# Moving the embedding projection of a one-core transformer-layer kernel from its last stage into its routing stage

## What is computed

```python
def channel_and_ple(x, p, g_ffn, w_rg, b_rg, w_re, b_re, w_gate, w_up, w_down, g_ple, w_ple_gate, w_ple_proj):
    h = rmsnorm(x, g_ffn).reshape(B * S, D)
    x = x + hier_moe(h, w_rg, b_rg, w_re, b_re, w_gate, w_up, w_down).reshape(B, S, D)
    e = (p.astype(x.dtype) @ w_ple_proj) * jax.nn.sigmoid(rmsnorm(x, g_ple) @ w_ple_gate)
    return x + e
...
y_prompt = rmsnorm(xp, final_norm_g)
```

## Time and profile before

| quantity | value |
|---|---|
| profiled execution | 2257.42 us, span 2255.6 us |
| median of the three runs | 2261.59 us |
| PE busy | 1997.7 us (89% of the span) |
| DVE, ACT, POOL busy | 1129.8, 867.4, 238.2 us |
| routing stage (e) | 1401.8 to 1431.5 us of the span |
| last stage (h) | 2064.6 to 2255.6 us of the span |

### The profile page before, as it was taken

How to read it: one execution, slowest core, us unless ns; L and a number is a source line. 1 busy time by engine, 2 the same in 40 slices (tenths; PEclk the granted TensorE clock), 3 DMA queues, 4 the chain that set the end, 5 groups by cost and what they waited for, 6 DMA issues and landing times. The chain is left out here.

```text
span 2255.6 us, 26518 instructions
## 1 busy us (share of the span) xinstructions
PE 1997.7 (89%) x9556; PEld 1633.7 (72%) x9556; DVE 1129.8 (50%) x1339; ACT 867.4 (38%) x1014; POOL 238.2 (11%) x232
## 2 busy tenths in 40 slices
PE   7889999965999999997999895499999999993887
PEld 5767888854777777786788684377777777773676
DVE  4224333324232233211643432789999999994443
ACT  4222000011332333322421211477777777773443
POOL 0000111122000000000222000100000000002232
PEclk9999999987999999987999897699999999996999
DMA  8426111197777545465333336399999999985231
GB/s 286 154 103 233 52 61 60 40 322 255 259 260 265 205 156 187 151 216 199 150 126 110 118 112 253 138 339 397 390 394 396 392 395 391 397 308 208 99 119 68
DMA packets 190913, 494.02 MB, mean 219 GB/s; under 512 B 16512, under 2 KB 32384, under 8 KB 180352
## 3 DMA queue, kind: packets, MB, share of 16 engines
q1 hardware_dynamic: 180128, 457.69, 55.4%
q0 software_dynamic: 7200, 26.22, 3.2%
q10 hardware_dynamic: 3520, 9.25, 1.1%
HBM read 402.94 MB, written 90.18 MB: 219 GB/s over the span
## 5 line engine op out<-in xcount | busy, mean ns | idle before, releaser
L2223 DVE TENSOR_TENSOR expert_w_rounded<-arena,expert_w_rounded 128x2048 fp32r<-128x2048 f32 x192 | 431.7, 2288 | 47.8 <-ACT expert_w_rounded L2180 47.8
L2180 ACT ACTIVATE expert_w_rounded<-arena 128x2048 fp32r<-128x2048 f32 x192 | 360.1, 1912 | 60.6 <-PE psum L162 39.1
L160 PE MATMUL psum<-expert_w_rounded,expert_x_rounded 128*128 128x512 f32 x768 | 312.1, 406 | 34.2 <-DVE expert_x_rounded L2236 27.1
L162 PE MATMUL psum<-expert_w_rounded,expert_x_rounded 128*128 128x512 f32 x768 | 303.1, 395 | 0.0
L161 PE MATMUL psum<-expert_w_rounded,expert_x_rounded 128*128 128x512 f32 x768 | 302.1, 393 | 0.0
L160 PE MATMUL psum<-host_w_rounded,host_x_rounded 128*128 128x512 f32 x432 | 195.1, 452 | 15.1 <-ACT arena L888 8.2
L160 PEld LDWEIGHTS psum<-expert_w_rounded,expert_x_rounded 128*128 128x128 f32 x768 | 146.2, 190 | 75.3 <-issue 36.8
L162 PE MATMUL psum<-host_w_rounded,host_x_rounded 128*128 128x512 f32 x432 | 175.3, 406 | 0.0
L161 PE MATMUL psum<-host_w_rounded,host_x_rounded 128*128 128x512 f32 x432 | 174.8, 405 | 0.0
L162 PEld LDWEIGHTS psum<-expert_w_rounded,expert_x_rounded 128*128 128x128 f32 x768 | 145.8, 190 | 32.4
L161 PEld LDWEIGHTS psum<-expert_w_rounded,expert_x_rounded 128*128 128x128 f32 x768 | 146.4, 191 | 28.3
(11 more groups left out here) (288 smaller groups left out, 3654.8 us busy)
## 6 DMA issues: line engine op xcount, KB each, us to landing
arena<-w_gate_e SPq DMA_DIRECT2D x32, 2048.0 KB, 9.6
arena<-w_up_e SPq DMA_DIRECT2D x32, 2048.0 KB, 10.6
arena<-w_down_e SPq DMA_DIRECT2D x32, 2048.0 KB, 9.4
host_x_rounded<-hx_scratch SPq DMA_DIRECT2D x54, 1024.0 KB, 5.4
y_scratch<-arena SPq DMA_DIRECT2D x49, 512.0 KB, 9.7
arena<-w_in SPq DMA_DIRECT2D x10, 2048.0 KB, 10.3
z_scratch<-arena SPq DMA_DIRECT2D x54, 256.0 KB, 2.1
arena<-x_all SPq DMA_DIRECT2D x18, 512.0 KB, 4.7
```

What stands on the lines that cost most here:

```text
L160: nc.tensor.matmul(out, x_hi, w_hi, start=first, stop=False)
L162: return nc.tensor.matmul(out, x_lo, w_hi, start=False, stop=last)
L2180: nc.scalar.activation(c.exact(his[n][:, half, :]), halves[b][n][:, half, :], ACT.Copy).then_inc(*w_hi_ready[n].inc)
L2223: nc.vector.tensor_tensor(c.exact(raw), raw, c.high(his[n][:, half, :]), ALU.subtract).then_inc(*w_lo_ready[n].inc)
```

## The change

1. The projection `p @ w_ple_proj` is done in stage e, for all nine tiles: PE transposes and multiplies, ACT rounds and evicts, POOL subtracts, and ACT's own DMA queue stores the result in a new scratch tensor `emb`. Its weight and all of `p` are loaded and the weight is split in stage d. PE puts tiles 0 to 2 ahead of the count matmuls, 3 to 6 between them and the selection, 7 and 8 behind it.
2. Stage d issues its last two stores first and then only two of the six expert loads. The other four are issued at the start of stage e.
3. Stage h loads `emb` (512 KB for each tile) in place of `p` (128 KB). Its loops are written out. `combined` runs one tile further ahead (in iteration t for tile t+1), with three buffers for `x2`; the norm of t+1 is made in iteration t too. `x` keeps two buffers, and SP's order stays load(t+2), `f_ready(t)`, store(t).

```diff
             sp.wait_ge(*wo_done(NT - 1))
-            for n, (dst, src, sem) in enumerate(first):
-                if n == 1:
-                    turn(NT, 1, False, True)
+            turn(NT, 1, False, True)
+            for dst, src, sem in c.first_experts[0:2]:
                 sp.dma_start(dst, src.rearrange("(k p) n -> p k n", p=P)).then_inc(sem, 16)
...
         @block.sync
         def _(sp):
             s.credit(sp)
+            for dst, src, sem in c.first_experts[2:]:
+                sp.dma_start(dst, src.rearrange("(k p) n -> p k n", p=P)).then_inc(sem, 16)
...
+            p_high(0)
             act.wait_ge(*exp_in(0))
             nc.scalar.activation(gexp, g4, ACT.Exp).then_inc(*gap_exp.inc)
-            act.wait_ge(*gap_ready(0))
-            nc.scalar.activation(gap, gap, ACT.Exp).then_inc(*gap_exp.inc)
+            for t in range(NT):
+                if t + 1 < NT:
+                    p_high(t + 1)
+                if t == 2:
+                    act.wait_ge(*gap_ready(0))
+                    nc.scalar.activation(gap, gap, ACT.Exp).then_inc(*gap_exp.inc)
+                evict(t)
+            act.wait_ge(*emb_stored(NT - 1, 0))
+            act.wait_ge(*emb_stored(NT - 2, 1))
...
+                nc.gpsimd.tensor_tensor(c.exact(pT[:, b]), pT[:, b], c.high(pT_hi[:, b]), ALU.subtract).then_inc(*p_lo_ready.inc)
...
+            def embedded(t):
+                b = t % 2
+                if t + 1 < NT:
+                    rows_transposed(t + 1)
+                pe.wait_ge(*p_lo_ready(t))
+                pe.wait_ge(*emb_out(t - 2))
+                for h in range(2):
+                    cols = slice(h * BANK, (h + 1) * BANK)
+                    for k in range(KP):
+                        last = split_product(nc, ps[:, 4 + 2 * b + h, :], c.exact(pT_hi[:, b, k, :]), c.exact(pT[:, b, k, :]),
+                                             c.w_pp_hi_x[:, k, cols], c.w_pp_x[:, k, cols], k == 0, k == KP - 1)
+                last.then_inc(*emb_done.inc)
...
+            for t in range(NT):
+                if t + 2 < NT:
+                    load(t + 2)
                 sp.wait_ge(*f_ready(t))
-                sp.dma_start(row(c.o["y_all"], t), out[:, b]).then_inc(*out_stored.inc(b))
-            in_pairs(sp, NT, tile, peel=3)
+                sp.dma_start(row(c.o["y_all"], t), out[:, t % 2]).then_inc(*out_stored.inc(t % 2))
...
+                dve.wait_ge(*emb_in(t, t % 2))
+                dve.wait_ge(*gate_out(t, h + 1))
+                nc.vector.tensor_tensor(e[:, cols], g[:, cols], emb[:, t % 2, cols], ALU.mult).then_inc(*e_ready.inc)
+                dve.wait_ge(*e_ready(t, h + 1))
+                dve.wait_ge(*f_ready(t - 1))
+                nc.vector.tensor_tensor(x3[:, cols], e[:, cols], x2[:, t % 3, cols], ALU.add).then_inc(*x3_ready.inc)
...
+            for t in range(NT + 1):
+                if t:
+                    embedded(t - 1, 0)
+                if t + 1 < NT:
+                    combined(t + 1)
+                if t < NT:
+                    transposed(t)
+                if t + 1 < NT:
+                    mean_square(t + 1)
+                if t:
+                    embedded(t - 1, 1)
...
+            for t in range(NT + 1):
+                if t:
+                    gated(t - 1, 0)
+                if t < NT:
+                    high(t)
+                if t + 1 < NT:
+                    square(t + 1)
+                    normalized(t + 1)
+                if t:
+                    gated(t - 1, 1)
```

More of the change, by code:

```diff
@@ L1998, in _ @@
             nc.tensor.matmul(ps[:, 1, 0:NT * NE], T["ones"], rows, start=True, stop=True).then_inc(*counted.inc)
+            for t in range(3, 7):
+                embedded(t)
             for n in range(TOP * NT):
@@ L2003, in _ @@
             last.then_inc(*ids_done.inc)
+            for t in range(7, NT):
+                embedded(t)
         @block.vector
@@ L2553, in turn @@
-            def turn(t, b, new, old):
-                if new:
-                    combined(t, b)
-                if not old:
-                    w_lo(range(3, len(pieces)))
-                if old:
-                    embedded(t - 1, 1 - b, 0)
-                if new:
-                    dve.wait_ge(*gate_done(t - 2))
-                    dve.wait_ge(*emb_done(t - 2))
-                    transposed(t, b)
-                if old:
-                    embedded(t - 1, 1 - b, 1)
+                dve.wait_ge(*emb_in(t, t % 2))
```

268 lines of the change are left out of this document (139 added, 129 removed).

## The result

| | median, us | lowest to highest | profiled execution | its span |
|---|---|---|---|---|
| before | 2258.11 (20 runs) | 2255.41 to 2264.47 | 2257.42 | 2255.6 |
| changed | 2262.44 (20 runs) | 2259.39 to 2270.9 | 2264.53 | 2262.7 |

The ratio is 1.0019, with an interval of 1.0011 to 1.0027: 0.2% slower, inside the 0.3% that the prediction called no change. The prediction was 2277 us, 2263 to 2292, with a chance of 0.81 for slower. The direction was right, but by the prediction's own bound of 0.3% this is its third rival, "the same", to which it gave 0.07, and not the slower kernel to which it gave 0.81. The waits and their order came as described; the size did not: on the profiled executions the change costs 7.1 us and not 15.6. The median of before was also 3.5 us lower over 20 runs than over the 3 to which the prediction added its sum.

A forecast was written before the change was run, and what follows sets the result against it. The prediction held that no engine is full and a ring of waits bounds stage h's turn. Routing 1.2 us later plus stage h 14.4 longer made 15.6, added to the median of 2261.59: 2277 us, range 2263 to 2292.

The forecast's parts named there:

- third rival: Whole kernel: landing at 3.4 us (7 less) and routing 6 less leave 2.6 us, 2264, within the bound; chance 0.07.
- barrier before routing: End of stage d: with fewer loads issued before the barrier, routing starts at 1387.0, a gain of 14.8 us.
- stage e: Routing stage: with the projection in it, it takes 45.7 us with its barrier, where it took 29.7.
- six turns: Stage h, iterations 2 to 7: each waits for its load of x, 6 x 21.3 = 127.8 us.
- The ring: Stage h: chain of waits per turn, with the load of x behind the store that waits for POOL's gain; 21.0 us.
- PE's path: Stage h: PE starts a gate half slow after nearly 7 us idle, half 7.9 us; with handover a turn takes 21.3.
- sign for the ring: Stage h: DVE would idle some 5 to 6 us before `combined`, with the load of `x_scratch` as releaser.
- The low end: Stage h: a landing of x at the shortest, 3.4 us, gives 7 us less.
- the uncovered case: Stage d: the weight split before DVE's first residual, costed at nothing, would be 2 us if uncovered.
- POOL's subtracts: Routing stage: they slow DVE's chain by 0.5 us for each of four, 2 us, between 0 and 4.
- the page's rule alone: Routing stage: by the skill's exclusion rule, nine subtracts could each hold DVE for their full length, some 7 us.
- second rival: Routing stage: PE stays at half clock, tiles cost 5.5 us in place of 3.2, 18 us more, 2295; chance 0.08.

The follow-up runs named there:

- experiment 1: Changed kernel with SP's load of x(t+3) issued ahead of its wait for the gain in the last stage; 2239.08 us, ratio 0.9925.
- experiment 4: Changed kernel with expert 1's three loads issued only after tile 6 of the projection; 2266.83 us, ratio 1.0037.
- experiment 8: Changed kernel with all six expert loads issued in stage d, as in the kernel before; 2281.91 us, ratio 1.0094.
- experiment 5: The kernel of experiment 1 with two buffers for x3; 2239.98 us, ratio 0.9914.
- experiment 6: The kernel of experiment 5 with the next tile's first sigmoid ahead of the scaling n3 on ACT; 2240.85 us, ratio 0.9918.
- experiment 9: Kernel before with late expert loads, early tile and early x load, and the projection in PE's idle time in the last stage; 2223.33 us, ratio 0.9846.
- experiment 2: Kernel before with only the late issue of expert loads (stores first, four loads moved to stage e); 2241.52 us, ratio 0.9925.
- experiment 3: Changed kernel with the last stage's order of before, combined(t) in iteration t, still loading emb; 2247.72 us, ratio 0.9961.

## Why the prediction was wrong

Every term of the sum, on the profiled executions:

| term | predicted, us | measured, us |
|---|---|---|
| stage d, the weight's load and split | 0 | +1.7 |
| barrier before routing | -14.8 | -15.2 |
| stage e | +16.0 | +15.1 |
| stages f and g | 0 | +0.1 |
| first sigmoid of stage h, beyond that | +2.0 | +1.8 |
| iteration 1, sigmoid to sigmoid | 15.1 long | 14.7 long |
| six turns | 127.8 long | 119.6 long |
| from there to the last gain | 23.3 long | 23.1 long |
| whole execution | +15.6 | +7.1 |

**The step that failed is the size of the turn**, "With the handover I take 21.3 for a turn". It measured 19.9. Two things are in this. The ring, which the prediction had at 21.0, measured 19.8; and the prediction then took PE's path, 21.3, as the bound, where PE was on no chain that set the turn. The waits, their order and their places were as described, and experiment 1, which takes that one wait away, gives 21 us back. From the gain at 2134.93 to the next at 2154.69, with a for the sigmoid at 2135.01:

- From the gain's start to `combined` it is 6.96 us, not 7.6. SP issues the load 0.40 us after the gain's end, not 0.78, and it lands in 4.14 us, not 4.5. The 0.78 holds 0.26 us between SP's two issues in the old loop and a load of `p` that the new one doesn't have. Why the landing was shorter no run shows; the medians are 4.3 us (3.8 to 5.6) here and 4.5 (3.4 to 5.1) before. Over the six turns this part is 6.9 to 7.5 us.
- From `combined` to ACT's high parts it is 4.47 us, not 4.67; the norm to the second half's sigmoid 2.97, not 3.15; from there to `x3` 2.14, where 2.1 was foretold; the final norm and POOL's start 3.22, not 3.45. The sum is 19.8 in place of 21.0.
- PE starts the half at 2147.20, 1.1 us ahead of the prediction, and needs 7.9 us from there with its handover, where 8.0 was foretold, the first ten matmuls at the slow pace. ACT's sigmoid of that half is at 2155.11, 0.49 us late for PE, but POOL's gain at 2154.69 did not wait for it. In four turns this sigmoid waited 0.16, 0.49, 0.84 and 1.11 us for PE, and the gains behind them still came 19.7 to 19.9 us apart.

That makes 1.4 us in the mean of six turns, 8.2 us of the 8.5 by which the sum was off. An error in a turn counts six times: issue and landing, less the 0.06 that the gain took longer, are 0.7 us in a turn and 4 us in the whole, a quarter of the forecast of 15.6.

Two of the prediction's own readings were loose, too. Its sign for the ring was DVE idle for "some 5 to 6 us" before `combined`; it was 3.3 to 3.8 us. Its own numbers give 3.9 (`x3` done at a + 4.0, `combined` at a + 7.9), and part of that time the product fills, which is held by the gain. And the gain of 3.15 us is 0.81 over 2.34; 0.88 is what line 2521 had left.

**The low end was there and got too little weight.** The prediction gave "a landing at the shortest here, 3.4" as 7 us less, which is a turn of 20.2. The measured turn lies past that end, but by several small parts: the landings were 4.1 to 4.6 us in the six turns, and none was as short as 3.4. The base, a median of three runs, was 3.5 us too high as well. On the base of 20 runs the same sum would have given 2274 and a range from about 2260, in which 2262 lies. The rest is the spread between executions: the profiled one of the kernel before lies 0.7 us below its median and that of the changed kernel 2.1 above, so that the medians are 4.3 us apart and the profiled executions 7.1.

**Stage d was not free.** DVE, "before DVE's first residual, where PE has a tile's matmuls to do", waits 4.20 us for ACT's half of the split and then takes 2.29:

```profile
1261.62 2.29 DVE L1906 TENSOR_TENSOR embed_w_rounded<-arena,embed_w_rounded 128x2048 fp32r<-128x2048 f32 x1 [4.20 <-ACT embed_w_rounded L1852]
...
1265.70 0.68 DVE L1879 TENSOR_TENSOR arena<-psum,arena 128x512 f32<-128x512 f32 x1
```

The residual that started at 1262.61 before starts at 1265.70. DVE was early there by less than the split takes, and I had not looked at how much. The stage ends 1.7 us later, about the 2 that the text named for the uncovered case. That this split is the whole of the 1.7 was not tried by itself, and the size varies: from the split of `out_w` to routing's first instruction it is 137.0 to 137.8 us in the four traces without the new split, 137.8 to 137.9 in three with it and 139.3 to 139.7 in five with it. So it costs from almost nothing to some 2 us.

**Routing was right in its sum, not in all its parts.** With three tiles ahead of it the count came 14.7 us into the stage, against 15.4. But PE was not the whole reason. DVE, on its way to the count, waits 3.93 us for ACT, which does its second exponential (line 2034) only behind the evictions of the first two tiles, and then only 0.50 us for PE:

```profile
1401.06 0.70 DVE L2118 TENSOR_SCALAR arena<-arena 128x9 f32<-128x9 f32 x1 [3.93 <-ACT arena L2034]
```

The prediction had no term for this order on ACT, and no run changed it. From the count to the end of the selection's inputs it took 16.8 us, not 15.2: the chain was slowed by 1.6 us, where the prediction took 2 for POOL's subtracts, and the 7 that it worked out by the page's rule alone did not come. PE left the slow clock after six matmuls and not after twelve, so the second rival was far off. The stores landed in 6.6 us (median) and not 2.9, with the expert loads in the queues beside them; ACT waited for them three times, 2.81, 3.46 and 3.84 us. But experiments 4 and 8 show that these waits cost nothing: the selection and what comes behind it bound the stage. This error lay on a way that didn't matter. The store's 2.9 at the stage's end was a little short too; 3.63 us pass there.

The Trainium skill, DMA: Bandwidth & Descriptors, "Queues, rings and completion order", says that each DMA engine takes turns between the queue rows it has work for, a packet at a time. The traces agree as far as the sharing goes: with all four expert loads in the queues the stores took 6.6 us (median), in experiment 4, where three came late, 4.6, and in experiment 8, with none, 2.6. That it goes by packets no run here shows.

**The port.** In the table of the turn the product of line 2613 takes 2.16 us beside the gain. The prediction had the gain held by DVE (up to 5 us more) and not DVE by the gain. In the changed kernel that hold costs nothing, for DVE then waits on `x` anyway; in experiment 1 the product is recorded 1.65 us longer, and experiments 5 and 6 show that neither a buffer nor a new order removes the hold. Not all of it is lost: `x3` waits for the gain anyway, so that the turn is 0.5 us shorter without it (experiment 9). The Trainium skill, SBUF — State Buffer, "Who interferes with whom", says that this exclusion needs two SBUF inputs on VectorE, and that an instruction with at most one, outside the 2-port performance modes, does not contend. By that rule, the traces agree: with both inputs in SBUF the product takes 1.20 to 2.44 us in the changed kernel and always ends 0.53 to 0.55 us after the gain does; with one in PSUM it takes 0.69 us beside a gain of the same length (experiment 9). So staging the projection in memory had a price that no term named: it turned a free product into a held one.

**Where the gain of a large change went.** The late issue brings 15 to 17 us (experiments 2 and 8). The projection's move costs 15.1 us in routing and up to 2 in stage d, while some 7 come back in the last stage, most of them with the table loads (from SP's first load there to the last gain it is 185.6 us before and 178.5 in experiment 3). The early tile, in the order as written, costs 13 and would give 8 with one load moved up. Together that is 4 to 8 us slower; the profiled executions say 7.1 and the medians 4.3.

## What to carry over

When an operation is moved a turn earlier, look first at which queue entry now has to come a turn earlier too: here one load behind a store on SP made a gain of 8 us a loss of 13. A large change that measures as no change is worth taking apart, since a part of 15 to 17 us was in it, hidden by two that cost. Work for an engine that idles inside its loop can be free: with twelve matmuls in the gap the turn was 15.9 us, without them 16.4, while the nine tiles' projection cost 15 us as work of its own in the routing stage. And a busy share or a mean clock that moves says nothing yet about the turn: PE went to 79 of 82 us at the full clock, and what made the turn shorter was a product that no longer stood behind POOL's gain. The chain that ended last shows which of the two it is.

## What the runs showed of the hardware

- PE's clock can fall after the work has begun. In experiment 6, behind 3.22 us of idle time, the first matmuls from 2134.59 on are 0.23 us apart (2.4 GHz), those from 2136.47 to 2139.03 0.43 apart (1.2 GHz; the granted clock of 2136.50 to 2139.40 is 0.50), and then 0.23 again (1.00). Behind the same idle time, 3.22 to 3.23 us, the next turn kept the full clock throughout (from 2151.53), and the one after it was slow at once (from 2166.84). With this kernel's order a slow half makes 16.9 us out of 15.3 for a turn; in experiment 1 halves at 0.50, 0.70 and 1.00 left the turn at 16.4. In the changed kernel, behind 5.88 us, the first ten start slow at once (granted clock 0.50 from 2147.20 to 2151.60, 1.00 from 2152 on):

```profile
2147.20 0.79 PE L160 MATMUL psum<-ple_w_rounded,ple_x_rounded 128*128 128x512 f32 x1 [5.88 <-DVE ple_x_rounded L2601]
```

- A DVE instruction held by POOL's gain is longer in the profile (2.3 for 0.69, 3.42 for 1.28 us); it does not show as idle time, and the product of line 2613 ends 0.5 us after the gain. POOL's gain is longer too when DVE is at work beside it: 2.66 us in experiment 6, and 2.92 to 3.48 in the long turns of the kernel before, for 2.34.
- An issue of a 2 MB load on SP can take long with such loads ahead of it: in the kernel before 0.40 us for the first and 0.43 for the second, then 2.98, 0.85, 10.95 and 5.11. DVE stood idle for 15.57 us in front of the barrier behind them.
